# Eight cache slots taken out of the retention stage, and the sample group's FFN doubled up for six steps

## The reference

```python
h = _rmsnorm(x, norm1_w) * (1 + sc1) + sh1
rq, rk, rv, rg, mq, mk, mv = jnp.split(h @ w_in, SPLITS, axis=-1)
ret_out, ret_s = _retention_branch(...)       # 8 heads of 64, in chunks of 128 tokens
#   att = (qc kc^T) * dmat ; o = att vc + (qc s) * q_dec ; s = s * c_dec + (kc * k_dec)^T vc
#   o is centred and scaled by its variance per head, times silu(rg)
moba_out = moba_mix(mq, mk, mv)               # block-sparse attention; the sample group's reads
                                              # all 32 cache pages of each of its 8 sequences
x = x + g1 * (concat([ret_out, moba_out]) @ w_out)
h2 = _rmsnorm(x, norm2_w) * (1 + sc2) + sh2
x = x + g2 * ((silu(h2 @ w_gate) * (h2 @ w_up)) @ w_down)
```

## Time and profile before

| | |
|---|---|
| runs | 1021.92 us median of 3 (1020.92 to 1023.32) |
| profiled execution | span 1019.3 us from first to last instruction; the profile has no other time for it, and what lies around the span is not in it |
| PE | busy 957.3 us, 94% of the span |
| DVE | 601.7 us, 59% |
| ACT | 337.1 us, 33% |
| POOL | 139.4 us, 14% |
| mean granted TensorE clock | 0.982 |
| HBM | 260.04 MB read, 5.64 MB written |

### The profile page before, as it was taken

The page is one execution under the profiler, slowest core; times in us unless marked ns, Lnnn a source line. Parts: engine busy times, 40 slices in busy tenths (PEclk is TensorE's granted clock), DMA queues, the critical chain, the costliest instruction groups (busy, mean ns, idle before and its releaser), DMA issues.

```text
span 1019.3 us, 20941 instructions
## 1 busy us (share of the span) xinstructions
PE 957.3 (94%) x7951; PEld 680.3 (67%) x7951; DVE 601.7 (59%) x1021; ACT 337.1 (33%) x733; POOL 139.4 (14%) x129
## 2 busy tenths in 40 slices
PE   3889999999999979899998999999999999999996
PEld 1567776766776545467756676766777777777775
DVE  1665765676576578776796674422666555453244
ACT  5411243335334426442242242432342222121113
POOL 0020113333100132224151220000000000000000
PEclk9999999999999999999998899999999999999998
DMA  9997779889777999979889579778477898787652
GB/s 340 374 354 266 275 268 314 286 268 290 260 255 229 330 373 346 370 255 329 312 304 326 173 254 285 217 215 275 120 206 204 224 232 236 217 251 246 205 188 88
DMA packets 217973, 269.13 MB, mean 264 GB/s; under 512 B 13474, under 2 KB 168426, under 8 KB 209683
## 3 DMA queue, kind: packets, MB, share of 16 engines
q1 hardware_dynamic: 111266, 127.70, 39.2%
q10 hardware_dynamic: 97392, 73.00, 23.6%
q0 software_dynamic: 9216, 67.11, 17.5%
HBM read 260.04 MB, written 5.64 MB: 261 GB/s over the span
## 4 chain that ended last, share of the span: by engine, by line
PE 76%; DVE 9%; DMA 7%; SPq 3%; issue 2%; DVEq 2%; ACT 1%; ACTq 0%
PE banks L1153 14%; PE banks L1154 13%; PE banks L1155 13%; PE banks L1106 6%; PE banks L1241 5%; PE banks L1166 4%; PE banks L1186 4%; PE banks L1168 4%; PE banks L1167 4%; DVE KT L1891 4%; DMA K<-in_cache_k,kidx 3%; DMA ctr<-in_const 1%; PE banks L1365 1%; DMA V<-in_cache_v 1%; DMA rawm<-in_w_mod 1%
## 5 line engine op out<-in xcount | busy, mean ns | idle before, releaser
L673 ACT ACTIVATE whi<-raw 128x1024 fp32r<-128x1024 f32 (+1 forms) x76 | 78.7, 1035 | 303.1 <-PE banks L1155 152.8
L1891 DVE STREAM_TRANSPOSE KT<-K 128x2048 f32<-128x2048 f32 x63 | 145.5, 2309 | 32.5 <-PE banks L1186 16.4
L1153 PE MATMUL banks<-ahi,whi 128*128 128x512 f32 x400 | 163.0, 408 | 1.0 <-DVE alo L1847 1.0
L1154 PE MATMUL banks<-alo,whi 128*128 128x512 f32 x400 | 157.1, 393 | 0.0
L1155 PE MATMUL banks<-ahi,rawlo 128*128 128x512 f32 x400 | 156.9, 392 | 0.0
L1854 DVE TENSOR_TENSOR rawlo<-raw,whi 128x1024 fp32r<-128x1024 f32 (+1 forms) x76 | 91.2, 1200 | 49.9 <-ACT whi L673 47.3
L538 POOL DMA_INDIRECT K<-in_cache_k,kidx x64 | 64.0, 1000 | 404.9 <-DVE KT L1891 357.4
L1153 PEld LDWEIGHTS banks<-ahi,whi 128*128 128x128 f32 x400 | 75.7, 189 | 30.8 <-issue 12.5
L1166 PE MATMUL banks<-ahi,whi 128*128 128x512 f32 x216 | 89.4, 414 | 1.9 <-DVE rawlo L1861 1.6
L1186 PE MATMUL banks<-KT,qbd 128*32 128x128 f32 x2048 | 74.0, 285 | 16.4 <-DVE KT L1891 14.5
L1155 PEld LDWEIGHTS banks<-ahi,rawlo 128*128 128x128 f32 x400 | 75.8, 189 | 16.8
(11 more groups left out here) (338 smaller groups left out, 1481.0 us busy)
## 6 DMA issues: line engine op xcount, KB each, us to landing
V<-in_cache_v SPq DMA_DIRECT2D x168, 256.0 KB
zT<-in_cache_v SPq DMA_DIRECT2D x56, 256.0 KB
raw<-in_w_in ACTq DMA_DIRECT2D x12, 1024.0 KB
rawm<-in_w_mod ACTq DMA_DIRECT2D x11, 1024.0 KB
raw<-in_w_gate ACTq DMA_DIRECT2D x22, 512.0 KB
raw<-in_w_up ACTq DMA_DIRECT2D x22, 512.0 KB
srw<-in_w_gate SPq DMA_DIRECT2D x22, 512.0 KB, 5.7
srw<-in_w_up SPq DMA_DIRECT2D x22, 512.0 KB, 7.3
```

The source lines that it names most:

```text
L673: act.activation(whi[t % 2][:, 0:kd, :], raw[u][:, 0:kd, t % 2 * P:(t % 2 + 1) * P], ACT.Copy).then_inc(s_hi, 1)
L1153: pe.matmul(out[:, :], whi[t % 2][:, k, :], hi(k), start=(first and n == 0), stop=False)
L1154: pe.matmul(out[:, :], whi[t % 2][:, k, :], lo(k), start=False, stop=False)
L1891: dve.transpose(KTb[:, :, :, :], Kb[g % 2][:, :]).then_inc(s_kt, 1)
```

## The change

**Slots and steps are no longer the same number.** `slots_of(step)` says which slots a step carries. Steps 0 to 27 carry their own. In the retention steps only seven slots remain: 28, 29, then 30 to 33 one for each head pair (in its third step) and 34 in step 42. From step 43 on a step carries the slot eight behind it (`BEHIND`). Because eight slots are one sequence, the small once-per-sequence steps meet the same prompt steps as before, one sequence later. From step 76 to 79 a step carries two slots (68 to 75: only values are left then). `S_END` goes from 76 to 80.

**The head pairs.** The one slot left stands after the key-value product and directly ahead of the outputs. Scores, turned keys and turned outputs come one after another; the copy of the outputs gets a place of its own (`ro_kept`), so that it no longer shares one with the scaled keys. On ACT the copies follow in a new order, on DVE the variance stands after the states.

**Six steps with two units.** The sample group's FFN has 22 units. The first twelve are made two to a step (`units_of`, `PAIRS = 6`) in steps 88 to 93, the others one to a step, with a second `xtmp` and a second half of `asm`. `S_FFN` goes from 84 to 88, `S_DOWN` from 106 to 104.

**The rings.** Slots 19 to 22, 24, and 48 to 52 now all use the one ring `VB`; slots 23, 25 to 47 (odd) and 53 on (odd) use others. The last of these lies where the turned keys were and waits for the last key product.

```diff
+BEHIND = NGRP
+SLOT_IN_RET = {NT: 28, NT + 1: 29, R_PAIR + 2: 30, R_PAIR + 5: 31, R_PAIR + 8: 32, R_PAIR + 11: 33, R_HEADS: 34}
+TWO_FROM = NG + 4
+def slots_of(step):
+    if step < NT:
+        return (step,)
+    if step < R_OUT:
+        return (SLOT_IN_RET[step],) if step in SLOT_IN_RET else ()
+    s = step - BEHIND
+    if s < TWO_FROM:
+        return (s,)
+    s += s - TWO_FROM
+    return (s, s + 1) if s < NG + LAG else ()
...
-S_END = NG + LAG
+S_END = BEHIND + TWO_FROM + (NG + LAG - TWO_FROM) // 2
-S_DOWN = S_FFN + FT
+PAIRS = 6
+units_of = lambda i: () if i < 0 else (2 * i, 2 * i + 1) if i < PAIRS else (PAIRS + i,) if PAIRS + i < FT else ()
+S_DOWN = S_FFN + FT - PAIRS
-RING_2 = {17: 7, 18: 1, 20: 5, 21: 1, 23: 5, 24: 1, 26: 1, 27: 5}
-RING_2.update({1: 6, 3: 6})
-RING_2.update({g: 2 if g < 32 else 3 if g < 53 else 4 for g in range(29, NG, 2)})
+RING_2 = {1: 6, 3: 6, 17: 7, 18: 1, 23: 2}
+RING_2.update({g: 3 for g in range(25, 48, 2)})
+RING_2.update({g: 4 for g in range(53, NG, 2)})
...
+            if hp < 2:
+                ret_scores(hp)
+                if hp == 1:
+                    turn_x(2)
+                turn_ret_keys(hp)
+                if hp:
+                    turn_out(hp - 1)
+            else:
+                turn_ret_keys(hp)
+                turn_out(hp - 1)
+                ret_scores(hp)
...
-            act.activation(scr[:, 3, :], SB[:, :], ACT.Copy).then_inc(s_roe, 1)
+            act.activation(ro_kept[:, :], SB[:, :], ACT.Copy).then_inc(s_roe, 1)
...
-            if 0 <= n < FT:
+            for n in units_of(s - S_FFN):
                 pe.wait_ge(s_sev, N_FFN + n + 1)
                 streamed(4 + n, (VO, DB)[n % 2], lambda k: asT[:, k, :])
```

More of the change, by code:

```diff
@@ L591, in _, with next_keys @@
         gather(1)
-        for g in range(2, NG):
+        def next_keys(g):
             pool.wait_ge(s_kt, g - 1)
             gather(g)
+        for g in range(2, R_PAIR):
+            next_keys(g)
             if M_TURN <= g - 4 < M_TURN + 2 * HP:
@@ L713, in keep_probs, with slot @@
             last.then_inc(s_te, 1)
[L715 to L722 removed]
+        def slot(step):
+            for s in slots_of(step):
+                b, t = s // NGRP - 1, s % NGRP
+                if 0 <= b < NB_SEQ and t == 3 and b != B_NORM:
+                    exps(b)
+                if 0 <= b < NB_SEQ and t in (4, 5):
+                    keep_probs(b, t - 4)
+                if s < NG and s % 4 == 3:
+                    keep_logits(s // NGRP, s % NGRP // 4)
         for k in range(KT):
@@ L891, in _ @@
             s = R_PAIR + 3 * hp
-            slot(s)
             if hp >= 2:
@@ L1256, in fold, with slot_head, slot_values, slot_tail @@
             pe.matmul(MI[0:32, 128:128 + HD], C("sum_pv"), sm[:, 832:896], start=True, stop=True).then_inc(s_oe, 1)
-        def slot_head(s):
-            if s < NG:
-                keys(s)
-            if NGRP <= s <= NG and s % NGRP == 0:
-                own_keys(s // NGRP - 1)
-        def slot_values(s):
-            if 0 <= s - LAG < NG:
-                weigh(s - LAG)
-        def slot_tail(s):
+        def slot_head(step):
+            for s in slots_of(step):
+                if s < NG:
+                    keys(s)
+                if NGRP <= s <= NG and s % NGRP == 0:
+                    own_keys(s // NGRP - 1)
+        def slot_values(step):
+            for s in slots_of(step):
+                if 0 <= s - LAG < NG:
+                    weigh(s - LAG)
+        def slot_tail(step):
+            for s in slots_of(step):
+                tail_of(s)
+        def tail_of(s):
             b, t = s // NGRP - 1, s % NGRP
@@ L1273, in slot_tail @@
                 turn_own(b)
-            if tail and t == 0 and not R_PAIR <= s < R_HEADS:
+            if tail and t == 0 and b != B_RET:
                 block_gates(b)
@@ L1286, in slot_tail, with slot_rest @@
                 fold(b - 1)
-        def slot_rest(s):
-            if s % NGRP == 4:
-                slot_tail(s)
-                slot_values(s)
-            else:
-                slot_values(s)
-                slot_tail(s)
+        def slot_rest(step):
+            for s in slots_of(step):
+                if s % NGRP == 4:
+                    tail_of(s)
+                if 0 <= s - LAG < NG:
+                    weigh(s - LAG)
+                if s % NGRP != 4:
+                    tail_of(s)
         def early_mod(n):
@@ L1470, in turn_out @@
             pe.wait_ge(s_roe, hp + 1)
+            if hp:
+                pe.wait_ge(s_roc, hp)
             for c in range(TT):
-                last = pe.matmul(DB[:, c * P:(c + 1) * P], scr[:, 3, c * P:(c + 1) * P], C("centre"), start=True, stop=True)
+                last = pe.matmul(DB[:, c * P:(c + 1) * P], ro_kept[:, c * P:(c + 1) * P], C("centre"), start=True, stop=True)
             last.then_inc(s_rot, 1)
```

231 lines of the change are left out of this document (109 added, 122 removed).

## The result

The changed kernel takes 1056.06 us (median of four runs, 1053.45 to 1060.57) against 1021.81 (1020.92 to 1023.32): ratio 1.0325, 95% interval 1.029 to 1.0361. It is slower by 34 us, where +2.1 was forecast with 1030 as the upper end. The profiled execution is the one of 1053.45 us.

A forecast was written before the change was run, and what follows sets the result against it. PE, busy 94% of 1019.3 us, was taken as the bound, with the retention stage held by its slots. -26.8 + 19.2 + 8.7 + 1.0 = +2.1 us gave 1024.0 us; forecast 1022.5 to 1027, range 1013.5 to 1030.

The forecast's parts named there:

- The retention stage: From 353.85 us to the first output tile: 58.7 us against 85.55, 26.8 us less, bounds 54 and 64.
- The slots back in the FFN: Eight slots moved beside FFN tiles at 2.4 us each: 19.2 us more (17 to 20.4).
- the exchange: Retention stage against FFN: 26.8 us less for five slots remaining, 19.2 us more for the eight moved.
- The rings and the doubled value slots: One ring for slots 49 to 52 and 20 to 22, 2 MiB of values in steps 76 to 79: 1.0 (0 to 3).
- The first tiles of the FFN with eight more gathers beside them: Start of the FFN: a wait appearing there was named as a sign the prediction would be wrong; no size.
- The doubled steps: Six steps with two sample units, PE waiting for weights: 7.0 + 2.5 - 0.8 = 8.7 us more, bounds 1 and 13.
- The two full waits of "3.0": Doubled gaps into steps 90 and 92, after odd tiles: PE's second chunk late by 3.0 us in full.
- under the same DMA waits: Steps 90, 92, 94: DVE's longer chain would make PE wait some 0.6 us, under the DMA waits.
- clock and order: Doubled steps: clock falls after 3 us waits cost 2.5 us; fewer changes between kinds of matmul give back 0.8.
- rival: Three: faster, streams not disturbing each other, 1016.3 (0.30); longer pair chain in the retention stage, 1029.3 (0.14); near-tie (0.18).

The follow-up runs named there:

- e9: Changed kernel with the 1 MiB state store in four parts (steps 62, 64, 66, 68) and the x2s load in step 69; 1044.45 us, ratio 1.0235.
- e3: Changed kernel with one value slot per step to the end, steps 76 to 83, what follows the last slot four steps later; 1039.45 us, ratio 1.0188.
- e4: Changed kernel with the pages of value slots 58 to 63 loaded for half their rows, as many transfers; 1051.82 us, ratio 1.0316.
- e11: Changed kernel with GpSimd issuing two of the four pages of each value slot 58 to 63 on its own queue; 1046.92 us, ratio 1.0265.
- e7: Changed kernel with its last twelve value slots as one, two, one, two over steps 72 to 79; 1044.09 us, ratio 1.0191.
- e13: Changed kernel: store in four parts, x2s later, GpSimd sharing pages from slot 54, two doubled sample steps, value slots one and two in turn; 1025.24 us, ratio 1.0043.
- e6: Kernel before with only the six doubled sample steps of the change, value slots left one per step; 1038.42 us, ratio 1.0173.
- e10: Changed kernel with the up weights of the sample FFN units issued by GpSimd on its own queue; 1056.21 us, ratio 1.0347.
- e12: Changed kernel: store in four parts, x2s later, GpSimd issuing half the pages of slots 58 to 63, two doubled sample steps (88, 89); 1027.55 us, ratio 1.0071.
- e8: Changed kernel with value slots one and two in turn, x2s load seven steps later, two doubled sample steps (91 and 97); 1036.1 us, ratio 1.015.

## Why the prediction was wrong

**The retention stage** was right: 58.7 forecast from 353.85 us, 58.35 measured; the first output tile starts at 412.20, and between 409.1 and 419.3 in the other executions with this part unchanged (439.35 and 442.05 where it is that of before). That it is right to 0.4 us is luck, because two differences cancel. The keys of step 29 and the stage's first scores in the changed kernel:

```profile
353.21 1.08 PE L1220 MATMUL banks<-KT,qbd 128*32 128x128 f32 x32
...
357.51 1.16 PE L1534 MATMUL banks<-zT 64*128 64x128 f32 x16
```

Before, the keys of step 29 start at 349.55 and the stage at 353.85. So the stage starts 3.7 us later and lasts 54.7, 4.0 less than laid out: 8.75 us of waits in place of 11.7, and 42.6 of work (45.94 busy less 3.3 for the clock, 0.94 on the mean) in place of 43.6. From the keys of step 29 to the first output tile it is 59.0 us here, 59.2 to 65.0 in the twelve other executions with this part unchanged (median of all 61.3), and 89.9, 88.3 and 87.5 in the three of before: 27 less by the medians, which is the forecast. PE's waits in the stage, most of them at places laid out; the one for V was not:

```profile
PE banks L1220 <- DVE KT L1932: 2.4, 2, 2.2
PE banks L1243 <- DVE sm L1975: 1.7, 1, 1.7
PE banks L1572 <- ACT sq_ret L894: 1.6, 2, 1.3
PE banks L1275 <- DMA V<-in_cache_v: 1.1, 1, 1.1
PE banks L1572 <- ACT scr L936: 0.9, 1, 0.9
```

But the gain is smaller than it looks. The stage had 12.07 us without PE work, and has 8.75 now: 3.3 us are gained in gaps, 23.9 in busy time, nearly all of it work that moves. The sum treated this rightly (-26.8 + 19.2 = -7.6), but with too small a price for the return.

**The slots back in the FFN**, 19.2 with 20.4 as the upper bound, cost some 22. Eight keys with their small steps are 10.7 us from tile 60 to 72 (98.0 in e9, of which up to 1.2 are waits, against 87.3 before). Eight values with theirs are 11.9 from tile 72 to 84 (83.5 in e3 against 71.6, which is tiles 72 to 76 of before, 26.67, and eight tiles alone at 5.62). So the exchange without any side loss is worth 5 us, not 7.6.

**The step that failed is "The rings and the doubled value slots"**: "At the 395 GB/s of the earlier trace rows that and half a MiB of weights take 6.6 us of a step of 8.2, so it just fits. I take 1.0 (0 to 3)." The cost was 15.2 us (e3). I priced eight pages by their bytes. They are paced by SyncE, which issues one in 1.11 us, and in no less with half the bytes (e4), 8.9 us for the eight; two issuers (e11) or an average of six pages a step (e7) take half or more of it back. What remains of it, 6 to 7 us there and some 4 with both (e13), is not pinned down; pages that land late behind the prompt's weights (e4) and waits too short to show (e7) are seen. The row to price it by was in the trace of before, SyncE's queue in the retention stage:

```profile
363.81 3.63 SPq L423 DMA_DIRECT2D V<-in_cache_v  x4
```

Four pages in 3.63 us, the last issue 0.33 of it, are the same 1.10 us a page. The working did not use it.

**Not in the sum at all**: tile 64 and the next, 7.3 us (e9). "The first tiles of the FFN with eight more gathers beside them" was named as a place where a new wait would make it wrong, and given no price. ScalarE's hold of 6.98 us was in the trace of before, hidden; the working has no term for it.

**The doubled steps**: the mechanism was right (waits for `srw`, the low clock behind them, 292 GB/s), the size not: 8.7 forecast, 16.7 alone on the kernel before (e6), 14.6 in the changed kernel. The two full waits of "3.0" are there, in the gaps ahead of tiles 91 (2.58) and 93 (1.03 and 2.48), and the gap between them has none, as worked out. What was too small: the waits in all, 10.4 us in e6 against 7.0, since VectorE's chain, put "under the same DMA waits", comes in other gaps or ahead of them (1.32 ahead of tile 90, 0.80 ahead of 93); and clock and order, 6.3 against 2.5 - 0.8. The rule of the Trainium skill (DMA: Bandwidth & Descriptors, Specifications) that was weighed there, 512 bytes for line rate, would have made this term 1; the trace does not agree, 291 and 299 GB/s with pieces of 512 bytes in e10's comparison, as the row had it.

**The exchange**: with all three losses mended the change is 0.4 to 0.7% slower, not 7.6 us faster. By e13's windows against before's: to the first output tile -21.9 us, to tile 60 -2.4, to tile 80 +22.8, behind it +6.3, together +4.8. With the 3.7 us that moved behind tile 80, the slots cost 26.5, their 22 of work and some 4 that the pages still cost, and the two doubled steps 2.6.

That the first stretch took 63.6 us in this execution and 58.4 in that of the changed kernel, 5.3 more, can be followed in the two traces, though no code before tile 43 differs: 2.4 are there before the stage (keys of step 29 at 355.59 instead of 353.21), 1.0 is one wait for a value page (2.16 after 1.13), and behind it e13 has a fall of the clock that the other has not, 1.7 (granted clock 0.51 from 388.40 to 391.80 us, 1.00 in the other). Executions scatter so. Whether a mended version can win at all stays open: the exchange is worth 5 us, and the pages and two doubled steps alone cost more than that in e13.

The measured time lies outside the range for two causes that no rival had, a rate of issue (14.2 us beyond its term) and a hold that lost its cover (7.3), with the doubled steps (5.9 beyond) and the moved slots (some 3) undersized beside them.

## What to carry to other kernels

Price a transfer three ways before you double it: bytes over the measured rate, issues times the interval on the queue that issues them, and what stands behind it on that queue. Where a stage is freed of work that is done elsewhere instead, only its idle time is gained; the work returns, and where it returns the engine had no gap and each covered hold (an issue of 7 us that nobody waited for) may lose its cover. Where steps are doubled to catch up, put them at the start of a stream, where its buffers are full (two pairs, 5.0 us in e12; 5.1 for each amid it in e8), or spread them, so that the mean stays within the rate of issue (e7).

A view of waits has a floor: it can miss a wait that is shorter than the record of the instruction ahead of it. Compare the length of the same stretch in two traces before you take a sum of waits for the loss.

## What the runs showed of the hardware

- A page load by an index read at run time follows the one before in 1.11 us on SyncE and 1.15 on GpSimd; with half the rows in 1.25, so fewer bytes do not issue faster. In the kernel before two loads of fixed address behind each other take 1.02 us on SyncE, the second issue 0.57 of it, so 0.45 apart; an estimate from these two is that some 0.66 of the 1.11 us is the reading of the address.
- A 128 KiB load behind a 1 MiB store in 256-byte rows held the issuing engine 7.0 us in the kernel before and 12.0 after, at 354 GB/s in the window around (589 to 605 us).
- Two streams of weights in 512-byte rows move 291 GB/s with one queue for the sample's and 299 with two.
- Waits of PE of 2.1 to 4.9 us in the FFN of the changed kernel each came with 3 to 7 us at or near the low level (granted clock 0.55 from 833.50 to 836.80, 0.50 from 607.80 to 614.60 around the wait of 4.86): 1.93 us for 32 matmuls that take 1.06 elsewhere.
